# Attention of the odd layer, placed among its query, key and value products

## The reference, cut to what matters

```python
h  = _rms(x, norm1_g[i]) * (1.0 + sc1) + sh1          # 512 tokens
hc = _rms(y, norm1_g[i]) * (1.0 + csc1) + csh1        # 256 context tokens
# _odd_mixer: 16 heads of 64
q, k, v = split(h @ w_in);  qc, kc, vc = split(hc @ w_in)   # q, k: RMS norm per head, times a gain
# _neighbourhood_attention: a token sits on a grid of 8 rows x 64 columns
s_nb = einsum(q_row, k_rows) * scale + bias           # neighbours within 16 columns, others masked
s_cx = einsum(q_row, k_ctx) * scale                   # all 256 context keys
p = softmax(concat([s_nb, s_cx]))
o = p[..., :n] @ v_rows + p[..., n:] @ v_ctx
x = x + g1 * (o @ w_out)                              # then norm 2 and the SwiGLU feed-forward
```

## Time and profile before

| what | us |
|---|---|
| median of 3 runs | 3950.31 (3944.05 to 3955.63) |
| the profiled execution | 3953.41 |
| its span, first to last instruction | 3951.6 |
| TensorE (PE) busy | 3690.2, 93% |
| VectorE (DVE) busy | 2085.7, 53% |
| ScalarE (ACT) busy | 1442.3, 36% |
| GpSimd (POOL) busy | 645.3, 16% |
| mean granted TensorE clock | 0.960 |

### The profile page before, as it was taken

The page is one execution under the profiler, slowest core; times in us unless marked ns, Lnnn a source line. Parts: engine busy times, 40 slices in busy tenths (PEclk is TensorE's granted clock), DMA queues, the critical chain, the costliest instruction groups (busy, mean ns, idle before and its releaser), DMA issues.

```text
span 3951.6 us, 50824 instructions
## 1 busy us (share of the span) xinstructions
PE 3690.2 (93%) x19794; PEld 2974.2 (75%) x19794; DVE 2085.7 (53%) x3730; ACT 1442.3 (36%) x2248; POOL 645.3 (16%) x651
## 2 busy tenths in 40 slices
PE   8889999999988999999999887999999979899999
PEld 6676677787766766777878765788888879777887
DVE  4646755766456366656664535355454252564333
ACT  3445643443133446424331325331112233552222
POOL 1110121212220011122122110113333122000000
PEclk9989999999989899999999897999999989999999
DMA  4111232323331111333233100112322111212222
GB/s 155 60 64 49 86 114 105 121 108 133 112 113 61 54 59 65 118 123 125 104 135 129 66 22 1 43 70 80 118 91 101 65 54 54 70 49 75 101 96 80
DMA packets 65808, 339.01 MB, mean 86 GB/s; under 512 B 6816, under 2 KB 8352, under 8 KB 39968
## 3 DMA queue, kind: packets, MB, share of 16 engines
q1 hardware_dynamic: 65568, 335.78, 23.6%
HBM read 327.36 MB, written 8.39 MB: 85 GB/s over the span
## 4 chain that ended last, share of the span: by engine, by line
PE 76%; DVE 13%; ACT 8%; issue 2%; POOL 1%; DMA 0%; DVEq 0%; ACTq 0%; POOLq 0%; SPq 0%
PE ps L1718 23%; PE ps L1720 22%; PE ps L1719 22%; DVE wl L1969 3%; PE ps L1707 3%; PE ps L1845 2%; ACT wh L1864 2%; PE ps L1727 2%; DVE tt L1977 1%; PE ps L1838 1%; DVE pb L2195 1%; DVE acc L1977 1%; DVE hl L1977 1%; ACT opb L1957 1%; DVE u L1969 1%
## 5 line engine op out<-in xcount | busy, mean ns | idle before, releaser
L1969 DVE TENSOR_TENSOR wl<-raw,wh 128x2048 fp32r<-128x2048 f32 (+2 forms) x275 | 554.9, 2018 | 402.9 <-ACT wh L1864 383.2
L1864 ACT ACTIVATE wh<-raw 128x2048 fp32r<-128x2048 f32 (+2 forms) x275 | 457.2, 1663 | 815.7 <-PE ps L1720 811.4
L1718 PE MATMUL ps<-hh,wh 128*128 128x512 f32 (+1 forms) x1248 | 449.3, 360 | 11.0 <-DVE hl L1977 9.4
L2218 POOL TENSOR_TENSOR lt<-lt,cs 128x1024 f32<-128x1024 f32 x96 | 188.2, 1960 | 1657.6 <-DVE acc L1977 1657.6
L1719 PE MATMUL ps<-hl,wh 128*128 128x512 f32 (+1 forms) x1248 | 444.8, 356 | 0.0
L1720 PE MATMUL ps<-hh,wl 128*128 128x512 f32 (+1 forms) x1248 | 444.8, 356 | 0.0
L1718 PE MATMUL ps<-xhb,wh 128*128 128x512 f32 x832 | 371.4, 446 | 13.6 <-DVE xlb L1969 10.9
L1719 PE MATMUL ps<-xlb,wh 128*128 128x512 f32 x832 | 338.2, 406 | 0.0
L1720 PE MATMUL ps<-xhb,wl 128*128 128x512 f32 x832 | 338.0, 406 | 0.0
L1718 PE MATMUL ps<-xha,wh 128*128 128x512 f32 x704 | 284.1, 404 | 14.6 <-DVE wl L1969 12.0
L1719 PE MATMUL ps<-xla,wh 128*128 128x512 f32 x704 | 281.6, 400 | 0.0
(11 more groups left out here) (264 smaller groups left out, 7323.3 us busy)
## 6 DMA issues: line engine op xcount, KB each, us to landing
raw<-in_wts SPq DMA_DIRECT2D x199, 1024.0 KB, 4.8
lt<-in_wts SPq DMA_DIRECT2D x110, 512.0 KB, 3.5
raw<-in_wts SPq DMA_DIRECT2D x44, 512.0 KB, 3.4
raw<-in_wts SPq DMA_DIRECT2D x28, 448.0 KB, 3.1
x_scratch<-xt SPq DMA_DIRECT2D x3, 2048.0 KB, 9.1
xt<-x_scratch SPq DMA_DIRECT2D x3, 2048.0 KB, 8.1
oe<-in_relb SPq DMA_DIRECT2D x16, 384.0 KB, 3.9
bt<-in_big SPq DMA_DIRECT2D x1, 2688.0 KB, 9.5
```

What stands on the lines that cost most here:

```text
L1718: T.matmul(u.out, u.sh, u.mh, start=u.first, stop=False)
L1864: A.activation(u.h, u.raw, ACT.Copy).then_inc(*act.inc())
L1969: V.tensor_tensor(o_, a, b, op).then_inc(*dve.inc())
L2218: G.tensor_tensor(o_, a, b, op).then_inc(*pool.inc())
```

## The change

The odd layer's panels are laid out anew: eight panels with 128 query and 128 key columns (head pair c), and after every second of them a value panel of 256 columns (head pairs c and c+1).

```diff
-    for q in range(12):
-        add((("oqkv", q), 1), 2048, lambda i, q=q: kcols(i["od_w_in_2"][0], np.arange(q * 256, q * 256 + 256)))
+    for c in range(8):
+        cols = np.r_[c * P:c * P + P, D + c * P:D + c * P + P]
+        add((("oqk", c), 1), 2048, lambda i, cols=cols: kcols(i["od_w_in_2"][0], cols))
+        if c in (0, 2, 4, 6):
+            add((("ov", c // 2), 1), 2048, lambda i, c=c: kcols(i["od_w_in_2"][0], np.arange(2 * D + c * P, 2 * D + c * P + 256)))
```

```diff
+                made = stages(pairs, PB, PTB, Ring(SA_), Ring(banks[6:7]), [[by] for _ in PB], [[] for _ in PTB])
+
+                def run():
+                    n = len(made)
+                    for t in range(n + 4):
+                        while t < n and not (ready[t // 4] and v_ready[t // 8]):
+                            yield
+                        for k0 in (0, 4):
+                            if 0 <= t - 3 < n:
+                                made[t - 3][2]([k0])
+                            yield
+                        if 0 <= t - 4 < n:
+                            made[t - 4][3]()
+                            made[t - 4][4]()
+                        yield
+                        if t < n:
+                            made[t][0]()
+                        if 0 <= t - 1 < n:
+                            made[t - 1][1]()
+                        yield
...
+                hook["rate"] = 4
+                for c in range(8):
+                    p = get((("oqk", c), 1), 8)
+                    firsts = first_tiles(p) if c == 0 else []
+                    run_later(turns, force=True)
+                    for i in range(6):
+                        b = firsts[i] if firsts and i < 4 else tile(p, i, 0 if i < 4 else P, 256)
+                        if i == 5:
+                            p.done(b.w)
+                        hd.push(b, b.w, i, 4 if i < 4 else 2, None, False, lambda b2, t2, c=c, i=i: place(c, i, b2, t2), False)
...
+                    if c % 2:
+                        continue
+                    q = c // 2
+                    p = get((("ov", q), 1), 8)
+                    for i in range(6):
+                        b = tile(p, i, 0, 256)
...
+                        v_t = evac(VV[q % 2][:, i, :], b.ap[:, 0:256], [b.w], free=[values_t[2 * q - 3]] if q > 1 else start)
+                        b.free = [v_t]
+                        hd.advance()
+                    v_ready[q].append(v_t)
+                    if q == 0:
+                        SA_[0].free = SA_[0].free + SA_[1].free
+                        hook["gen"] = run()
+                hook["rate"] = 12
+                while hd.row:
+                    hd.advance()
+                bring_back(0, 0, 2, [values_t[5], now("dve")[0]])
+                FR = Ring(banks[0:6])
+                p = get((("oo", 0), 1), 8)
+                bs = [FR.next(), FR.next()]
+                for k in range(8):
+                    if k == 7:
+                        finish_bg()
+                    while o_ks[k] is None:
+                        bg()
+                    for m, b in enumerate(bs):
+                        b.w = dense(b.ap, p.h[:, k, m * P:m * P + P], p.l[:, k, m * P:m * P + P], OH[:, k, :], OL[:, k, :],
+                                    k == 0, k == 7, k == 7, [o_ks[k]], *((p.w, b.free) if k == 0 else ()))
+                        step()
+                p.done(b.w)
+                bring_back(1, 2, 8, now("pe", "act"))
```

`ready[c]` is filled when the keys of the last tile of head pair c are placed, `v_ready` after a value panel. The one call per tile into the query and key buffers, and the order within `Heads.push`:

```diff
+                def place(c, i, b2, t2):
+                    if i < 4:
+                        for n0, a0, a1 in [(448, 0, 64), (0, 64, P)] if i == 0 else [(i * P - 64, 0, P)]:
+                            evac(QT[:, c, n0:n0 + a1 - a0], b2.ap[:, a0:a1], [t2, gq_t], scale=GQ)
+                    y = P if i < 4 else 0
...
+                    k_t = evac(KT[c % 2][:, i * P:i * P + P], b2.ap[:, y:y + P], [t2], scale=Q("odk"),
+                               free=[scored_t[c - 2]] if c > 1 else [by])
...
+                    if self.row and "d" not in self.row[-1]:
+                        self.scale(self.row[-1])
                     self.squares(x)
                     self.row.append(x)
-                    if len(self.row) > 1:
-                        self.scale(self.row[-2])
```

```diff
+            def put_by():
+                add("load", dst=xx_dram, src=XX[:, :, :].rearrange("p k n -> p (k n)"), sem=s_by, free=list(xr_t))
+
+            def bring_back(n, k0, k1, free):
+                add("load", dst=XX[:, k0:k1, :].rearrange("p k n -> p (k n)"), src=xx_dram[:, k0 * S:k1 * S], sem=s_back[n], free=free)
```

More of the change, by code:

```diff
@@ L1432, in tm_bank, with stages @@
                 return b, t
[L1434 to L1453, removed]
+            def stages(pairs, PB, PTB, SR2, AT2, pbf, ptf):
                 def pair(n, it):
@@ L1502, in pair, with attend @@
                     return s1, norm_, s2, s3, s4
-                made = [pair(n, it) for n, it in enumerate(pairs)]
+                return [pair(n, it) for n, it in enumerate(pairs)]
+            def attend(pairs, PB, PTB, wide):
+                S2 = [Bank(ps[:, wide * i:wide * i + wide, :].rearrange("p a n -> p (a n)")) for i in range(4 // wide)]
+                for i, b in enumerate(S2):
+                    b.free = sum((banks[wide * i + a].free for a in range(wide)), [])
+                n_ = now()
+                made = stages(pairs, PB, PTB, Ring(S2), Ring(banks[4:6]), [list(n_) for _ in PB], [list(n_) for _ in PTB])
                 for x_ in range(len(made) + 5):
@@ L1603, in odd @@
             def odd():
+                nonlocal FR
                 h_ks = norm(1, 1, True, True)
                 QT = buf("oqt", [P, 8, S], M0)
[L1606 to L1643, removed]
-                PTB = [buf(f"opt{i}", [P, 1024], M0 + 32768 + 1024 * i) for i in range(2)]
-                s_e = [sem(f"s_e{i}") for i in range(4)]
-                e_free = [w] * 4
-                zero_t = POOL(add("zeros", bufs=(E[:, 12, :],)))
+                OH = buf("oh", [P, 8, S], M0 + 4096, F32R)
@@ new lines, in odd @@
+                GQ = RS[:, 1, 0:1]
+                by = (s_by, 16)
+                gq_t = evac(GQ, Q("odq"), [prm], scale=SCALE)
+                s_e = [sem(f"s_e{i}") for i in range(4)]
+                start = now("pe")
+                e_free = [start] * 4
+                HR, SA_ = Ring(banks[0:3]), banks[4:6]
+                hd = Heads(Ring(banks[3:4]), QS, [by])
+                ready, v_ready = [[] for _ in range(8)], [[] for _ in range(4)]
+                scored_t, o_ks, values_t = [None] * 8, [None] * 8, [None] * 8
@@ L1651, in load_bias @@
                     add("load", dst=e_, src=relb[h], sem=s_e[h % 4], free=e_free[h % 4])
[L1653 to L1655 removed]
+                pairs = []
                 for c in range(8):
@@ new lines, in odd @@
+                            came=ready[c], v=[[vv[:, j, a:a + 64] for j in (i, (i + 1) % 4, 4, 5)] for a in (c % 2 * P, c % 2 * P + 64)],
+                            v_t=v_ready[c // 2], bank=banks[7], col=i * P, first=i == 0, last=i == 3, finish=finish))
+                made = stages(pairs, PB, PTB, Ring(SA_), Ring(banks[6:7]), [[by] for _ in PB], [[] for _ in PTB])
[17 more added lines that the diff above has]
+                        yield
```

120 lines of the change are left out of this document (86 added, 34 removed).

## The result

The changed kernel takes 4029.38 us (median of 4 runs, 4026.51 to 4032.05) against 3947.93 for the kernel before in the same session (4 runs): ratio 1.0204, 95% interval 1.0186 to 1.0222. It is 81 us slower. The forecast was slower, 3995 (own range 3970 to 4018); the time lies just above the upper end of the whole range, 4028.

The account below looks back on a forecast made before the run. TensorE's own work was taken as the bound, leaving 25 us of attention waits to win. Terms 20.2 - 15.4 + 30 + 15 - 6 + 0.8 gave +44.6, so 3995 on the median; own range 3970 to 4018, whole range 3958 to 4028.

Parts of the forecast that it names:

- What bounds the stage: Odd layer's attention: 100 of 125.4 us is TensorE's own work, so overlap can win only 25 us of waiting.
- Narrow tiles: Odd layer's query and key products: 384 matmuls of 128 columns at 0.1125 us replace 192 of 256 at 0.120, +20.2 us.
- Attention among products, -15.4: Odd layer's attention placed between dense matmuls: 32 pairs at 3.44 us, 110 us in place of 125.4.
- The wait for the copy: Second transposes in the overlap wait for ScalarE's copy out of single bank 6, behind two exponentials: 30 us together.
- The case where a panel ends: Three turns where a low-half subtraction of 2.29 us stands ahead of the bias add: +2.2 us each, 7 together.
- The tail: Pairs 28 to 31 after the last key tile, with little dense work between pieces: 15 us (ends 6 and 25).
- the last values: Sign in the trace after: last attention values some 15 us behind the last key tile's matmul, and idle there.
- Head turns, -6 and +0.8: Odd layer's waits for scaled heads: scaling before squares saves 6 of 7.0 us; the first two turned tiles lose 0.8.
- rival 3: TensorE's clock falls to 1.2 GHz for stretches because of strewn waits: +80 us, 4030; chance 0.13.
- the forecast's 44.6: Sum of all terms over the odd layer's rebuilt stage: 20.2 - 15.4 + 30 + 15 - 6 + 0.8 us.
- Rows to DRAM and back: Residual rows stored in the layer's norm and loaded back around the first output panel: taken as 0, between 0 and 1.

Follow-up runs that it names:

- run 4: The kernel before with only narrow context tiles (panels of 128 query and 128 key columns), attention behind the fence as before: 3970.6 us, ratio 1.0055.
- run 1: The changed kernel with the scores piece moved ahead of the values, so first transposes follow values: 3978.4 us, ratio 1.0075 to the kernel before.
- run 9: The kernel before with a waiting head tile scaled ahead of the next tile's squares, in both layers: 3958.2 us, ratio 1.0015.
- run 3: The kernel before with only the residual rows stored to DRAM and loaded back: 3950.7 us, ratio 1.0005.
- run 2: The changed kernel, old order of pieces, with transposes and head turns sharing banks 3 and 6: 4000.8 us, ratio 1.0132 to the kernel before.
- run 5: The changed kernel with 171 useless matmuls ahead of second transposes, in the wait's place: 4025.8 us, ratio 1.0196 to the kernel before.

## Why the prediction was wrong in size and right in kind

- **What bounds the stage: right.** "All that overlap can win here" was put at 25 us. In that stage of before TensorE waits 6.6 + 3.6 + 3.2 + 2.6 = 16.0 us, and 6.8 more are the clock's. The best overlap found wins 12, and only after the narrow tiles, the order, the bank and the even layer's heads are all mended.
- **Narrow tiles: right.** +20.2 forecast, +21.8 alone, starts 0.11 apart. The Trainium skill's page "TensorE: Matmul & The Clock Gate", section "Back-to-back issue gap", gives about 81 ns for 128 columns; the runs here show 112 (median of the 384 in run 4), so the row with 24 columns was the better guide.
- **Attention among products, -15.4: probably too small.** It was not measured alone. The sum of the stage closes with it only if the clock's loss in the stage of before is taken off twice; counted once, the five kernels with narrow tiles ask for about -20 to -22, or 103 to 105 us of work where 110 was forecast. Its bounds were 100 and 114.
- **The wait for the copy: right.** Place and cause are as forecast, and the size nearly: 30 us in the overlap and 7 in the tail forecast, 26.5 and 8.1 measured. Order alone takes away 26.8 of the 34.6 (run 1). The case where a panel ends, worked out from the earlier trace rows, is the chain at 3291.68 above.
- **The tail: right in its waits.** 15 forecast; from the last dense matmul with `hh` TensorE waits 4.9 + 0.5 for key copies, 8.1 for copies into `opt` and 3.0 for `ol`, 16.5. One sign failed: the last values come 51 us behind the last key tile's matmul (3552.4 to 3603.8), not some 15.
- **Head turns, -6 and +0.8: wrong, there is no gain.** Outside the tail the odd layer's waits at turns are 9.4 + 6.7 = 16.1, where it was 16.7 before and 11.5 was forecast. The waits for `u` did fall by 7.3, but turns now have one bank, whose key copy stands on ScalarE behind high halves and exponentials. And `Heads` serves the even layer too, which the prediction overlooked: there the new order costs 8.0 us of waits (10.7 to 18.7) and 5.6 us of time. Most of the 4.0 us ahead of the stage is of this kind: with the head order alone (run 9) the same point lies 3.4 us later.
- **The clock: this is the step that failed.** The forecast held no term for it; it was rival 3, at 0.13, argued against by the 0.99 of 3413 to 3507, "in spite of a wait in nearly every pair". Those waits are 0.43 us a pair. After, 28 waits for the copy average 1.2 us and reach 3.2, and the clock over the stage is 0.905 against 0.960: 25.6 us more than in the kernel before, and about 30 to 32 us more than the forecast had in it, whose 110 us of attention stood at full clock. Of the 51.2 us more at the lower level 10.2 are at the entry (0.67 over 31 us, where the kernel before has 0.83; run 4 has 0.67 too), the rest in the overlap and tail. Forecast and rival were not alternatives: the forecast's own 30 us of stalls bring the rival with them. The rival's 4030 is 1 us from the result, in part by luck: it gave the clock 35 us, and other terms make up the difference.
- **The account.** The waits of the stage in all were forecast well: +39.8 (30 + 15 - 6 + 0.8) against +42.5. So the forecast's 44.6, with 2.7 more of waits, 32.4 of clock, 6.8 less of attention, 4.0 ahead of the stage and 1.2 behind it, is 78.1, where the spans differ by 78.3. The 6.8 is fitted, not measured.
- **Rows to DRAM and back: right for the time.** TensorE did not wait for them and run 3 is level with the kernel before; but one residual on VectorE waited 4.6 us for its rows, where 0 to 1 was forecast.

## What to carry to other kernels

Before overlapping a stage, subtract the bounding engine's own work from its length: only the rest can be won, and narrower tiles or shared banks can cost more than that. Order interleaved pieces so that the copy which frees a bank is not queued behind a later piece's long work on the same in-order engine; here that order alone was worth 51 us. When a forecast contains many stalls of TensorE like these (28 of 1.2 us on average), price the clock that goes with them in the same sum: here 25.6 us on 42.5 of added waits (20.5 without the entry), 23.9 on 30.8 in run 1 and 11.9 on 16.5 in run 2, so 0.5 to 0.8 us for each 1 us. And look for every other user of a helper that is edited.

## What the runs showed of the hardware

- The clock's fall is a cost that useless work can buy back: 20 us of matmuls in the place of some waits, which took only 9.5 us off them, left the kernel no slower (4025.8 and 4029.4), the granted clock of the stretch going from 0.905 to 0.946 (run 5).
- Dense matmuls behind a wait of 1.72 us ran at 0.52 for 6 us, 37 starts; behind the same wait shortened to 0.71 us at 1.00, 58 starts (run 5).
- In the kernel before 94 us with a short wait in nearly every pair ran at 0.99; in the changed one 22 waits for the copy, of 1.2 us on average, left 0.93 over 318 us; with waits for that copy of 1.0 at most it was 1.00 over 272 us (run 1).
- A float32r matmul of 128 columns with its own weights takes 0.112 us from start to start (run 4), as one of 24 columns does (0.1125); 256 columns take 0.120.
